# Moving the tile that feeds the weight products by 8 bytes within SBUF

## What is computed

```
for layer in range(2):
    h = h + rms_norm(mixer(rms_norm(h) , ...))      # layer 0: gated recurrence (w_in 1024x4096, w_out 1024x1024)
                                                    # layer 1: differential attention (w_kv, w_q, w_out)
    ff = (relu(rms_norm(h) @ w_up) ** 2) @ w_down   # 1024 x 4096 x 1024
    h = h + rms_norm(ff)
...
h = rmsnorm(x);  z = h @ w_in                       # second block: 1024 x 2080
m = concat(rmsnorm(attention(z)), rmsnorm(gated_conv(z)))
x = x + rmsnorm(m @ w_out)
f = (silu(h @ w_gate) * (h @ w_up)) @ w_down        # 1024 x 2816 x 1024
x = x + rmsnorm(f);  x = x + sigmoid(x @ w_ple_gate) * rmsnorm(p @ w_ple_proj)
```

## Time and profile before

| | |
|---|---|
| median of 3 runs | 966.21 us (966.04 to 966.22) |
| profiled execution: span from first to last instruction | 963.2 us |
| its own time beside the span | not recorded apart; the median lies 3.0 us above the span |
| PE busy | 952.3 us, 99% |
| PE weight loads busy | 909.1 us, 94% |
| DVE, ACT, POOL busy | 748.2, 547.7, 89.4 us |
| chain that ended last | PE 82%, DVE 12% |
| granted TensorE clock | 0.999 of full speed |

### The profile page before, as it was taken

How to read it: one execution, slowest core, us unless ns; L and a number is a source line. 1 busy time by engine, 2 the same in 40 slices (tenths; PEclk the granted TensorE clock), 3 DMA queues, 4 the chain that set the end, 5 groups by cost and what they waited for, 6 DMA issues and landing times.

```text
span 963.2 us, 18430 instructions
## 1 busy us (share of the span) xinstructions
PE 952.3 (99%) x7530; PEld 909.1 (94%) x7530; DVE 748.2 (78%) x1129; ACT 547.7 (57%) x819; POOL 89.4 (9%) x91
## 2 busy tenths in 40 slices
PE   9999999999999999999999999999999999999998
PEld 8999999999999998999999999999999999999998
DVE  6998778978855599867987844489887998787777
ACT  6652366656454476756665544455666665556455
POOL 5334101000201000001000201001001000000000
PEclk9999999999999999999999999999999999999999
DMA  8733444766666836436476575626636467665651
GB/s 256 243 120 115 143 128 140 218 200 197 195 183 193 267 109 197 150 113 183 136 215 197 176 214 184 194 68 182 183 110 202 127 197 214 187 190 170 203 175 44
DMA packets 164723, 166.62 MB, mean 173 GB/s; under 512 B 6784, under 2 KB 162832, under 8 KB 164640
## 3 DMA queue, kind: packets, MB, share of 16 engines
q1 hardware_dynamic: 162752, 163.47, 55.5%
q0 software_dynamic: 1056, 1.19, 0.5%
q10 hardware_dynamic: 832, 0.79, 0.4%
HBM read 163.82 MB, written 1.08 MB: 171 GB/s over the span
## 4 chain that ended last, share of the span: by engine, by line
PE 82%; DVE 12%; issue 2%; ACT 2%; DMA 2%; SPq 0%; POOL 0%; ACTq 0%; DVEq 0%
PE ps L657 19%; PE ps L660 16%; PE ps L649 13%; DVE w_lo L1990 4%; PE ps L676 3%; PE ps L677 3%; PE ps L678 3%; PE ps L682 2%; PE ps L683 2%; PE ps L684 2%; PE ps L689 2%; PE ps L609 2%; PE ps L617 2%; PE ps L690 2%; PE ps L691 2%
## 5 line engine op out<-in xcount | busy, mean ns | idle before, releaser
L1990 DVE TENSOR_TENSOR w_lo<-w_raw,w_hi 128x1024 fp32r<-128x1024 f32 (+4 forms) x314 | 375.0, 1205 | 116.1 <-ACT w_hi L1424 110.3
L1424 ACT ACTIVATE w_hi<-w_raw 128x1024 fp32r<-128x1024 f32 x298 | 313.3, 1056 | 200.3 <-PE ps L660 47.6
L657 PE MATMUL ps<-xs,w_hi 128*128 128x256 f32 x1012 | 132.6, 277 | 0.0
L657 PEld LDWEIGHTS ps<-xs,w_hi 128*128 128x128 f32 x1012 | 127.0, 188 | 4.5
L660 PE MATMUL ps<-xs,w_lo 128*128 128x256 f32 x832 | 112.2, 277 | 0.0
L660 PEld LDWEIGHTS ps<-xs,w_lo 128*128 128x128 f32 x832 | 102.9, 188 | 0.2
L682 PE MATMUL ps<-xs,w_hi 128*128 128x256 f32 x320 | 91.4, 285 | 0.4 <-DVE w_lo L1990 0.4
L683 PE MATMUL ps<-xs,w_hi 128*128 128x256 f32 x320 | 89.3, 279 | 0.0
L684 PE MATMUL ps<-xs,w_lo 128*128 128x256 f32 x320 | 89.3, 279 | 0.0
L649 PE MATMUL ps<-xs,w_hi 128*128 128x512 f32 x326 | 85.1, 393 | 0.3 <-DVE mo L2018 0.2
L1431 ACT ACTIVATE tmp<-ps 128x512 f32<-128x512 f32 x75 | 44.5, 593 | 70.6 <-PE ps L649 62.6
(11 more groups left out here) (431 smaller groups left out, 1896.6 us busy)
## 6 DMA issues: line engine op xcount, KB each, us to landing
w_raw<-in_mlp_w_up SPq DMA_DIRECT2D x64, 512.0 KB, 4.2
w_raw<-in_mlp_w_down SPq DMA_DIRECT2D x64, 512.0 KB, 3.5
w_raw<-in_a_w_in SPq DMA_DIRECT2D x32, 512.0 KB, 4.3
w_raw<-in_w_gate SPq DMA_DIRECT2D x22, 512.0 KB, 3.8
w_raw<-in_w_up SPq DMA_DIRECT2D x22, 512.0 KB, 4.6
w_raw<-in_w_down SPq DMA_DIRECT2D x20, 512.0 KB, 4.4
w_raw<-in_w_kv SPq DMA_DIRECT2D x16, 512.0 KB, 4.3
w_raw<-in_w_in SPq DMA_DIRECT2D x16, 512.0 KB, 3.9
```

The costliest lines, as they stand in the source:

```text
L657: mm(ps[:, 2 * pset + n, at], hi[:, kk, n * P:(n + 1) * P], x[:, kt0 + kk, at], start=False, stop=False)
L1424: o = fn(dst, raw, ACT.Copy)
L1990: return v.tensor_tensor(d, x, y, ALU.subtract)
```

## The change

The tile `xs` is allocated as one row of 4100 elements instead of 8 x 512, and a view of it that leaves out the first two elements (8 bytes) and the last two takes the name `xs`. The 16 bytes more round its size up by 64, which replaces the 64 bytes of padding that stood behind it, so that every other tile stays at its address. All 8 feature tiles of `xs`, both parts, now start at 72 by 128, which is 8 by 16, where they started at 64, which is 0 by 16. Instructions, their shapes, their order and their waits are the same.

```
+HALF_LINE = 2
...
         h = sb("h", [P, KT, S])
         top[0] += HALF_PERIOD
-        xs = sb("xs", [P, KT, 2 * S], F32R)
-        top[0] += HALF_PERIOD
+
+        def shifted(t, n):
+            return t[:, HALF_LINE:HALF_LINE + n * 2 * S].rearrange("p (k n) -> p k n", k=n)
+
+        xs = shifted(sb("xs", [P, KT * 2 * S + 2 * HALF_LINE], F32R), KT)
         mo = sb("mo", [P, KT, S])
```

## The result

The changed kernel takes 983.5 us (median of 4 runs, 983.3 to 983.63) against 966.12 us: ratio 1.0182, interval 1.0168 to 1.0196. It is 17.4 us slower. The prediction said 962 us and a range of 955.5 to 972.

The account below looks back on a forecast made before the run. PE, busy 99% of the span, was taken as the bound. Half of the long matmuls on `xs` turning short saved 4.4 us, 963.2 to 958.8 us of span, plus 3.0 us to the median: 962 us, range 955.5 to 972.

Parts of the forecast that it names:

- the writers: ScalarE and VectorE passes that write `xs`, 510 and 478 ns: taken as zero change, kept at 0 to 1 us.
- the two paces of the earlier trace: 256-column matmuls on PE before the change: short 113.3 ns and long 117.9 ns, each kept over dozens of matmuls.
- The term of the sum: Streamed read of `xs` on PE: half of 1930 long matmuls turn short, 4.6 ns each, 4.4 us saved.
- The remark that DVE and PE take turns: From 30 to 131 us the recurrence alternates with products on the chain; a reason to count half the long matmuls.
- The counts: 256-column matmuls on `xs`: about 1930 taken as long and 1853 as short (wide ones among them).
- the 109 ns: Lower bound for the pace on `xs`: a weight load alone, from eight 128-column matmuls in 0.87 us.
- The 3.0 us beside the span: Added to the forecast span of 958.8 us because the median lies 3.0 us above the span, giving 961.8 us.
- The upper end: Slow-side bound on `xs`: one piece more per pass, 6.8 us, or all short matmuls turning long, 8.5 us; range top 972.
- One piece more per pass: Rival: each streamed read of `xs` touches 65 pieces in place of 64, 6.8 us slower, 973.0 us; chance 0.17.
- The paces swap: Rival: on `xs` short stretches turn long and long ones short, plus 4.1 us, 970.3 us; chance 0.16.
- Nothing: Rival: the address does not set the phase, paces stay as they are, 966.2 us within 1.5; chance 0.25.
- The far end of the forecast: All long matmuls turn short, 8.9 us, and 512-column ones gain 3 us: 954 us; chance 0.42 together with the forecast.

Follow-up runs that it names:

- the probes: Kernels of their own, none of the reference: PE runs rows of matmuls at chosen stream and weight starts; 64 and 0 (stream, weights) gave 117.8 ns in all nine rows.
- x112: `xs` at 112 by 128, against the kernel before with 64, weights still at 0: 966.19 us, ratio 1.0003.
- probe1: Kernel of its own, none of the reference: rows of 40 matmuls, one pair of starts each, other engines quiet; 64 and 0 (stream, weights) had 117.8 ns.
- x16: Changed kernel with a shift of 16 bytes in place of 8, `xs` at 80 by 128: 980.35 us, ratio 1.0154 against the kernel before.
- all32: Kernel before with weights moved to 32 and all activation tiles to 96 by 128, still 64 apart: 964.55 us, ratio 0.9986.
- The map: PE-only kernel, none of the reference: all pairs of stream and weight starts in steps of 16 bytes, two draws each; 113.3 ns at 5 pairs of 64.

## Why the prediction was wrong

**The bound was read rightly.** PE's pace on `xs` decides, nothing else moved: `us`, the writers and the other engines stayed, as priced. That the pace hangs on the address of the stream was right too. Which way it would go was a guess from half a piece of shift, and no row bore on it.

**The step that failed** is "I take it that the shift changes which of them a stretch settles in, and not the paces". The changed kernel shows on `xs` hardly anything of the two paces of the earlier trace rows but a third, 121 ns, and the probes show a whole set between 113 and 130 ns. The two paces of the trace belonged to one pair of places, 64 and 0, which is one of the few that can run at 113.3. Of six other places for `xs`, five lost that pace, whatever the size of the move: 4, 8 and 16 bytes and the whole 64 cost 14 to 17 us. The term of the sum should have been 3405 x 5.4 = 18.4 us up, not 4.4 us down.

**The gain would not have come either.** The prediction let half of the stretches at 118 turn to 113 and took the full 4.6 ns for each. x112 did that for more of them and won nothing: of its 4.8 us, 3.0 came back as waits and the other products lost 1.9. Of the nine waits that grew by 0.2 us or more in the profile of x112, six end on VectorE. The remark that DVE and PE take turns was right (DVE has 12% of the chain in the earlier trace rows), but was used to halve the gain and should have taken more of it.

**Smaller terms.** The counts were too high: the rows hold 512-column and turned products too. By the starts, 1585 of the 256-column matmuls on `xs` were long and 1820 short, so all long ones turned short would have been 7.3 us and not 8.9. The row behind the 109 ns is of plain float32 transposes and not of a weight load; the nearest to a `float32r` weight load alone are the rows of 64 columns in probe1, 111.7 ns. The 3.0 us beside the span set a profile against the median of other executions; within one run it is 1.8 us.

**The bounds.** The upper end was too near. It knew one piece more (1.8 ns) and a fall from 113 to 118 for the short ones; measured were 5.4 ns in the mean on 3405 matmuls, above both. No row gave a pace for another pair of places, and a bound taken from two values of the same pair was none.

**The rivals.** *One piece more per pass* had the sign and, with plus 6.8 us, the nearest price, but not the mechanism: its 115 ns on `xs` is not what was found. The Trainium skill, page SBUF — State Buffer, section Specifications, says that each cross to a new 16-byte line pays a penalty. The runs do not bear it out as the price of this change: x16, which starts at a line's edge, loses 14.9 us, 254 columns within 64 pieces were no better (120.0 and 117.8 ns), and 76 and 0, inside a piece, had 116.7 where 64 and 0 had 117.8. *The paces swap* had the sign too (plus 4.1) but the wrong picture: stretches that were long did not get shorter. *Nothing* is ruled out. The far end of the forecast, all at 113, was nearly reached by x112 on `xs`, and was worth no time there. all32, where `us` is short as well, won 1.4 us.

What stays open is the mechanism: why 113.3 ns is found at 64 apart for some places and at 112 and 0, but not at 64 and 80, which are as far apart, and what lets 64 and 0 find it in the kernel and not in the probes. The map is given as measured.

## What to carry to other kernels

If PE bounds a kernel and its `float32r` operands sit in hand-placed tiles, the starts of the streamed and the stationary tile by 128 bytes can be worth 6% of the pace (113 to 120 ns here, 1.8% of the kernel's time); read the start-to-start time in the order of time, and when one stretch shows the better pace, take a move of either tile as a loss until measured. Padding that looks idle, like the 64 bytes around `xs`, can carry this. A shorter pace pays only where PE isn't waiting for weights: check the waits behind it before counting it.

## What was not expected of the hardware

A `float32r` matmul with 128 stationary and 256 streamed columns has at least seven steady paces by the places of its operands (113.3, 116.7, 117.8, 118.3, 120.0, 121.2, 130.0 ns), for many pairs the same within 0.2 ns in four draws. In probe1 the granted clock, 1.00 from 215 to 219 us, fell during rows of 64-column matmuls that ran back to back at 111.7 ns. Two stretches of that kernel (us, PE busy and count, PEld, DVE, ACT, POOL, clock, DMA share, GB/s):

```profile
221.00:229.00 8.00, 8.00 (x50) 7.48 (x48) 0.00 (x0) 0.00 (x0) 0.00 (x0) 0.76 0.00 0
230.00:250.00 20.00, 20.00 (x86) 19.28 (x86) 0.00 (x0) 0.00 (x0) 0.00 (x0) 0.50 0.00 1
```

PE's records leave no gap there, and from 230 us the clock stood at 0.50 of full, the 1.2 GHz level, with a pace of 213.3 ns. In the rows of 256 columns that followed it was 0.88 (251 to 257 us) and then 1.00 (258 to 264 us). The 64-column rows with the weights at 8 were run at the lower clock and tell nothing of places.
